# Gated linear attention on one core: the samples' tile first, their state updates spread over the prompt's tiles, and the conditioning matmuls in four column quadrants with half of them ahead

## The reference, cut to what matters

```
mod = jax.nn.silu(c) @ w_ada + b_ada            # [9, 1024] @ [1024, 6 * 1024]
sh1, sc1, ga1, sh2, sc2, ga2 = split(mod, 6)
h = rms_norm(x, g_mix) * (1.0 + sc1) + sh1      # sh1, sc1 are needed first
... q, k, v, r, a_low = split(h @ w_in) ...
# gated linear attention, 4 heads, keys of 64, values of 128, state S [64, 128] a head
S   = exp(sum log_a) * S + sum_t k_t v_t^T
o_t = q_t S_t ;  o = rms_norm(o) * silu(r)
x = x + ga1 * (concat(o_sb, o) @ w_out)         # ga1 and the rest are needed after it
```

## Time and profile before

| what | us |
|---|---|
| median of 3 runs (lowest, highest) | 2003.95 (2003.08, 2006.66) |
| the profiled execution, its own time | 2010.14 |
| its span in the profile | 2008.1 |
| PE busy in the span | 1770.6 (88%) |
| DVE busy, ACT busy, POOL busy | 706.4, 565.6, 405.2 |
| `stage_start`, up to the first matmul of the next stage | 0 to 80.3 |
| `stage_gla` | 844 to 1057.5 |

### The profile page before, as it was taken

The page is one execution under the profiler, slowest core; times in us unless marked ns, Lnnn a source line. Parts: engine busy times, 40 slices in busy tenths (PEclk is TensorE's granted clock), DMA queues, the critical chain, the costliest instruction groups (busy, mean ns, idle before and its releaser), DMA issues. The chain is left out here.

```text
span 2008.1 us, 26856 instructions
## 1 busy us (share of the span) xinstructions
PE 1770.6 (88%) x10388; PEld 1513.1 (75%) x10388; DVE 706.4 (35%) x1302; ACT 565.6 (28%) x1087; POOL 405.2 (20%) x293
## 2 busy tenths in 40 slices
PE   7799789999946888878867967999999999999996
PEld 1599778788834444423446967999999999999996
DVE  2300122322215777656550133323232323233334
ACT  3411021111115777633322133121213121212122
POOL 1011121122110000100001123232324242323230
PEclk9799989999977999979868988999999999999998
DMA  8121354554173000155405101111111111111102
GB/s 299 54 86 55 92 180 140 159 162 126 54 252 121 22 22 1 47 152 157 134 16 183 42 0 45 62 42 42 42 42 42 42 42 59 45 42 42 42 0 100
DMA packets 102739, 164.97 MB, mean 82 GB/s; under 512 B 7498, under 2 KB 55965, under 8 KB 102662
## 3 DMA queue, kind: packets, MB, share of 16 engines
q1 hardware_dynamic: 93952, 133.71, 20.6%
q0 software_dynamic: 5120, 16.78, 2.7%
q10 hardware_dynamic: 3590, 13.48, 1.7%
HBM read 138.18 MB, written 25.76 MB: 82 GB/s over the span
## 5 line engine op out<-in xcount | busy, mean ns | idle before, releaser
L376 PE MATMUL psum<-op_hi,out_hi 128*128 128x384 f32 (+1 forms) x960 | 319.8, 333 | 29.7 <-DVEq L2232 29.7
L378 PE MATMUL psum<-op_hi,out_lo 128*128 128x384 f32 (+1 forms) x960 | 314.8, 328 | 0.0
L377 PE MATMUL psum<-op_lo,out_hi 128*128 128x384 f32 (+1 forms) x960 | 314.8, 328 | 0.0
L378 PE MATMUL psum<-mlp_a_hi,out_lo 128*128 128x384 f32 (+1 forms) x768 | 250.9, 327 | 0.0
L377 PE MATMUL psum<-mlp_a_lo,out_hi 128*128 128x384 f32 (+1 forms) x768 | 250.6, 326 | 0.0
L376 PE MATMUL psum<-mlp_a_hi,out_hi 128*128 128x384 f32 (+1 forms) x768 | 250.4, 326 | 0.0
L376 PEld LDWEIGHTS psum<-op_hi,out_hi 128*128 128x128 f32 x960 | 181.8, 189 | 31.8 <-DVEq L2232 30.2
L2189 POOL TENSOR_TENSOR out_lo<-out_raw,out_hi 128x2048 fp32r<-128x2048 f32 x31 | 143.1, 4615 | 273.6 <-ACT out_hi L2209 273.6
L2238 DVE TENSOR_TENSOR mlp_sq<-mlp_relu 128x384 f32<-128x384 f32 (+1 forms) x96 | 88.3, 920 | 296.4 <-ACT mlp_relu L2222 296.4
L377 PEld LDWEIGHTS psum<-op_lo,out_hi 128*128 128x128 f32 x960 | 181.8, 189 | 1.6
L378 PEld LDWEIGHTS psum<-op_hi,out_lo 128*128 128x128 f32 x960 | 181.6, 189 | 0.0
(11 more groups left out here) (291 smaller groups left out, 2856.3 us busy)
## 6 DMA issues: line engine op xcount, KB each, us to landing
sa_k<-in_cache_k SPq DMA_DIRECT2D x64, 256.0 KB, 3.1
sa_v<-in_cache_v POOLq DMA_DIRECT2D x64, 256.0 KB, 3.8
ada_w<-in_w_ada SPq DMA_DIRECT2D x32, 512.0 KB
out_raw<-in_w_up SPq DMA_DIRECT2D x16, 1024.0 KB, 5.4
out_raw<-in_w_down SPq DMA_DIRECT2D x16, 1024.0 KB, 5.1
ada_w<-in_w_ada SPq DMA_DIRECT2D x4, 2048.0 KB, 12.4
projT<-in_stage ACTq DMA_DIRECT2D x12, 544.0 KB, 2.7
projT<-pg_stage ACTq DMA_DIRECT2D x12, 544.0 KB, 4.0
```

The lines of the kernel that those rows point to most:

```text
L376: pe.matmul(out, w_hi, x_hi, start=(k == 0), stop=False)
L377: pe.matmul(out, w_hi, x_lo, start=False, stop=False)
L378: return pe.matmul(out, w_lo, x_hi, start=False, stop=(k == nk - 1))
```

## The change

- `cT` is padded to 32 columns a slice (`QUAD` = 32). `condition` lets input slice k write to the PSUM partitions `32 * (k % 4)` onwards: four slices sum into four quadrants of one bank, two each. DVE or ACT then copies all 128 partitions, and `turn_rows` no longer transposes but multiplies the 128 rows with `gather` (128 x 9, four identities one below the other), which adds the four quadrants while it turns. POOL makes `gather` and zeroes `cT` at the start.
- In `stage_gla` a quarter is 512 rows x 256 columns (512 KB as before, in rows of 1 KB where they were 2 KB). The first `PRE` = 4 chunks, 16 quarters, are loaded and multiplied before the loop, through 6 buffers: the two own ones and four that alias tiles the loop uses later. A quarter is loaded once the last one in its buffer is used (`SLOT`). Chunks 4 to 7 are done in the loop, in the samples' tile and the first three of the prompt, through the two own buffers, and in two halves: quarters 0 and 1 before `turn_out`, quarters 2 and 3 after it. The copy of the rows moves from DVE to ACT, to the end of ACT's work for a tile.
- The samples' tile comes first: position n = 0 is tile 8, position n is tile n-1. `keys(n)` is that of prompt tile n and feeds `score(n+1)`; `outer` and `state` of a prompt tile move to `outer(n-1)`, `state(n-1)`. The samples' values and keys have buffers of their own (`vs`, `kns`). SP loads `S0` and the first `r` and `v` tiles behind the 16 quarters.
- The samples' states are updated in pairs at n = 5 to 8: `mask_keys(pair)` on DVE, `sample_outer(pair)` on PE (8 matmuls of 64 x 64 x 128, was 4 of 64 x 128 x 256, for two samples), `sample_states(pair)` on DVE one position later. Only the last pair's update lies behind the loop.
- Elsewhere buffers are only overlaid to make room.

```diff
-def condition(pe, g, bank, w, k0, n):
+def condition(pe, g, bank, w, k0, n, cols=slice(0, 512)):
 
     for k in range(k0, k0 + n):
-        last = pe.matmul(bank[0:NMOD, :], g.cT[:, k, :], w[:, k - k0, :], start=(k == 0), stop=(k == KD - 1))
+        q = k % 4 * QUAD
+        last = pe.matmul(bank[q:q + QUAD, cols], g.cT[:, k, :], w[:, k - k0, :], start=(k < 4), stop=(k >= 4),
+                         skip_group_check=True)
     return last
 
 
 def turn_rows(pe, g, bank, c0, rows):
 
     for m in range(4):
-        last = pe.transpose(bank[:, c0 + m * NMOD:c0 + (m + 1) * NMOD], rows[:, m * P:(m + 1) * P], g.ident[0:NMOD, 0:NMOD])
+        last = pe.matmul(bank[:, c0 + m * NMOD:c0 + (m + 1) * NMOD], rows[:, m * P:(m + 1) * P], g.gather[:],
+                         start=True, stop=True, skip_group_check=True)
...
+        own = [sb(f"ada2_w{i}", [P, 4, 256]) for i in range(2)]
+        wa = [t[:] for t in own] + [t[:].rearrange("p a h t -> p (a h t)").rearrange("p (k c) -> p k c", k=4) for t in (pt2, on2, fin2, sr2)]
+        arow = [sb(f"ada2_rows{i}", [P, 512]) for i in range(2)]
...
+        PRE = 4
+        PAIR_AT = {5: 0, 6: 1, 7: 2, 8: 3}
+        SLOT = [t % 6 if t < 4 * PRE else t % 2 for t in range(4 * NADA)]
...
+        ADA = [g.bank[b] for b in (7, 6, 5, 4, 7, 7, 7, 7)]
...
+                for i in range(4 * PRE):
                     weights(i)
+                sp.dma_start(vs[:], g.vgnat[tile(NT)]).then_inc(s_vs, 16)
                 sp.wait_ge(s_z, 4)
                 s0d = io["state_gla"][0].rearrange("s (m h) k v -> h m k s v", h=2)
                 for h in range(2):
                     for m in range(2):
                         sp.dma_start(s0[HALF[h], :, 2 * m + h, :], s0d[h, m]).then_inc(s_s0, 16)
+                load_r(0)
+                load_v(0)
+                load_r(1)
+                load_v(1)
+                load_r(2)
+                for n in range(2, N9):
+                    for i in range(4 * PRE + 4 * n - 8, min(4 * PRE + 4 * n - 4, 4 * NADA)):
+                        weights(i)
+                    if n > 2:
+                        load_r(n)
+                    if n < NT:
+                        load_v(n)
...
+                def ada_rows(i):
+                    act.wait_ge(s_am, 4 * i + 4)
+                    at_least(act, s_at, i - 1)
+                    act.copy(arow[i % 2][:], ADA[i]).then_inc(s_ar, 1)
...
+                ada_rows(3)
                 copy_kn(0)
+                for n in range(N9):
+                    if n < NT:
+                        key_exps(n)
+                    if n + 1 < N9:
+                        copy_kn(n + 1)
+                    gate_ln(n)
+                    norms(n)
+                    gate_exp(n)
+                    if n > 0:
+                        fin_hi(n - 1)
+                    if n + PRE < NADA:
+                        ada_rows(n + PRE)
...
+                dve.wait_ge(s_kn, 1)
+                for n in range(N9):
+                    if n < NT:
+                        keys(n)
+                    scores(n)
+                    gate_exponent(n)
+                    if n > 0:
+                        normed(n - 1)
+                    for i in {0: (2, 3), 1: (4,), 2: (5,), 3: (6,), 4: (7,)}.get(n, ()):
+                        ada_mod(i)
+                    if n == 4:
+                        scale_gain(dve, g, g.mul2, SC2, KD)
+                    if n > 0:
+                        if n > 1:
+                            dve.wait_ge(s_st, 4 * n - 4)
+                        state(n - 1)
+                    if n - 1 in PAIR_AT:
+                        sample_states(PAIR_AT[n - 1])
+                    if n in PAIR_AT:
+                        mask_keys(PAIR_AT[n])
+                    if n > 0:
+                        gated(n - 1)
+                sample_states(PAIR_AT[NT])
                 normed(NT)
                 gated(NT)
...
+                def sample_outer(pair):
+
+                    pe.wait_ge(s_km, 2 * pair + 2)
+                    pe.wait_ge(s_ae, NADA)
+                    pe.wait_ge(s_x, 1 + 8 * pair)
+                    for s in range(2):
+                        for m in range(2):
+                            for h in range(2):
+                                head, c0 = 2 * m + h, (2 * s + m) * GV
+                                last = pe.matmul(XP[HALF[h], c0:c0 + GV], kem[s][:, head * GK:(head + 1) * GK],
+                                                 vs[:, head * GV:(head + 1) * GV], start=True, stop=True, skip_group_check=True)
+                    last.then_inc(s_xp, 1)
 
                 ada(0)
+                for i in range(1, PRE):
+                    ada(i)
+                    turn_ada(i - 1)
                 pe.wait_ge(s_d, 13)
                 turn_keys(0)
                 score(0)
+                turn_ada(PRE - 1)
+
+                for n in range(N9):
+                    if n + 1 < N9:
+                        turn_keys(n + 1)
+                        score(n + 1)
+                    if 0 < n <= NADA - PRE:
+                        turn_ada(n + PRE - 1)
+                    output(n)
+                    if n > 0:
+                        outer(n - 1)
+                    if n + PRE < NADA:
+                        ada(n + PRE, (0, 1))
+                    if n > 0:
+                        turn_out(n - 1)
+                    if n + PRE < NADA:
+                        ada(n + PRE, (2, 3))
+                    if n in PAIR_AT:
+                        sample_outer(PAIR_AT[n])
                 turn_out(NT)
```

More of the change, by code:

```diff
@@ L181, in stage_start @@
         w = [sb(f"ada_w{i}", [P, KD, 512]) for i in range(2)]
-        rows = [sb(f"ada_rows{i}", [NMOD, 512]) for i in range(2)]
+        rows = [sb(f"ada_rows{i}", [P, 512]) for i in range(2)]
+        spare = sb("ada_silu_den", [P, KD, NMOD])
         vec = sb("ada_vec", [VEC_B + 6 * KD, P])
         x = [sb(f"n1_x{i}", [P, D]) for i in range(9)]
-        sq = sb("n1_sq", [P, D])
+        sq = hT_lo[:, 0, 0:D]
         ss = sb("n1_ss", [P, 9])
@@ L246, in _ @@
                 pool.tensor_copy(g.ident16[:], g.ident[:]).then_inc(s_const, 1)
+                pool.memset(g.gather[:], 0.0).then_inc(s_const, 1)
+                pool.memset(g.cT[:], 0.0).then_inc(s_const, 1)
+                for q in range(4):
+                    pool.wait_ge(s_const, 7 + q)
+                    pool.affine_select(out=g.gather[:], in_=g.gather[:], compare_op=ALU.not_equal, fill=1.0,
+                                       base=-q * QUAD, pattern=[[-1, NMOD]], channel_multiplier=1).then_inc(s_const, 1)
                 w_in.first_lo(pool)
@@ L704, in stage_project_gla_and_sample_attention @@
         w = [sb(f"sa_w{i}", [P, NPAGE, 4, QUAD]) for i in range(2)]
-        orow = [sb(f"sa_out_rows{i}", [P, P]) for i in range(2)]
         o = g.sample_o
@@ L1437, in weights @@
-                    sp.dma_start(wa[i % 2][:], part.rearrange("(k p) c -> p k c", p=P)).then_inc(s_wa[i % 2], 16)
-                for i in range(2):
-                    load_r(i)
-                for i in range(10):
+                    half, k = divmod(m, 2)
+                    c0 = 2 * D + chunk * 512 + half * 256
+                    part = io["w_ada"][0][k * 4 * P:(k + 1) * 4 * P, c0:c0 + 256]
+                    sp.dma_start(wa[SLOT[i]], part.rearrange("(k p) c -> p k c", p=P)).then_inc(s_wa[SLOT[i]], 16)
@@ new lines, in sample_states @@
+                def sample_states(pair):
+                    dve.wait_ge(s_xp, pair + 1)
+                    for s in (2 * pair, 2 * pair + 1):
+                        for h in range(GH):
+                            r = HALF[h % 2]
+                            c0 = (s % 2 * 2 + h // 2) * GV
+                            dve.scalar_tensor_tensor(out=s0[r, s, h, :], in0=s0[r, s, h, :], scalar=dec[r, h // 2, NT + s:NT + s + 1],
+                                                     in1=XP[r, c0:c0 + GV], op0=ALU.mult, op1=ALU.add).then_inc(s_x, 1)
```

304 lines of the change are left out of this document (124 added, 180 removed).

## The result

| | before | after |
|---|---|---|
| time, median of 5 runs | 2004.98 us (2003.08 to 2008.22) | 2016.16 us (2014.62 to 2019.09) |
| ratio, 95% interval | | 1.0055 [1.004, 1.007] |
| profiled execution, its span | 2010.14, 2008.1 us | 2014.62, 2013.0 us |
| first matmul of `project_in` | 80.30 us | 77.70 us |
| gated attention, DVE's first step to the next stage's first load | 845.50 to 1057.56, 212.1 us | 839.75 to 1062.99, 223.2 us |

The forecast was 2000.8 us, in a range of 1983 to 2010. The change takes 61 us from the conditioning's matmuls: they were 101.7 us and are now 41.0 us in 320 records. (The page's group of 240 records and 30.7 us leaves out the 80 whose quarters lie in the four aliased tiles.) The turns of the rows take 13.8 us more, 18.9 for 5.1. And the kernel is slower.

What follows compares the result with a forecast made beforehand. PE was taken to bound the kernel, busy 88% of the span, conditioning matmuls holding 101.7 us. Opening -7.8 and gated attention +4.6 sum to -3.2, from a median of 2003.95 to 2000.8 us; range 1983 to 2010.

Steps and rivals of the forecast that it cites:

- the quadrants' speed: Conditioning matmuls: quadrants overlap fully for f32, so a chunk takes 1.8 us at full clock, 3.5 at low.
- that rival: Conditioning: quadrants do not overlap at 256 or 512 columns, the opening gains nothing, 2027 us; chance 0.04.
- The opening, -7.8: Opening stage: ACT starts modulating x at 42.3 instead of 50.1, a gain of 7.8 us.
- bias and multiplier 0.9: Opening stage, DVE after chunk 3's turn: bias and multiplier together take 0.9 us.
- The prologue: Gated attention before position 1: about 10 us later than the old loop's start, sample tile included; output(0) ends at 899.6.
- Positions with conditioning, 20.0 us: Gated attention, samples' tile and n = 1 to 3: 20.0 us a position for 16.6, keys waiting on ACT.
- The wait does not form: Gated attention, n = 1 to 3: quarters 2 and 3 come early, positions take 17.3 us, 1992; chance 0.15.
- quarters late: Gated attention: quarters 2 and 3 arrive later than 3.85 us; at 5.9 us it is +8, 2009; chance 0.17.
- Positions without it: Gated attention's later positions: keys 7.8 us after outer, burst 9.0; a pair's updates, 3.0 us, lie on DVE's chain.
- Clock credit, 4 us: Gated attention: the clock returns before outer ends in some bursts, 0.5 us each, 4 us taken off in all.
- My slower rival: Gated attention: quarters 2 and 3 arrive later than 3.85 us, each microsecond costing four on ACT's chain; chance 0.17.
- Clock rivals: Gated attention: full clock holds in half the bursts, 1983 us, chance 0.15, or in all, 1970 us, chance 0.04.

Runs made afterwards that it cites:

- The opening alone: Changed opening stage with the gated attention of the kernel before: 2001.24 us, ratio to before 0.9967.
- POOL waiting: Kernel after, with POOL's subtraction of the first w_in panel waiting until DVE has done the multiplier: 2015.65 us, ratio to before 1.0045.
- the fillers: Kernel after with conditioning rows copied later on ACT, plus unread matmuls where PE waits in the gated attention: 1988.42 us, ratio to before 0.9905.
- The last order: Kernel after with rows' copy later, POOL's wait, next keys earlier, late quarters and samples' outer products behind the next score: 1971.69 us, ratio to before 0.9822.
- The gated attention alone: Changed gated attention with the opening's product and turn in whole rows as before: 2023.98 us, ratio to before 1.0078.
- the early keys: Kernel before, with the next tile's keys ahead of the state update on DVE and their exponentials ahead of ACT's norms: 2018.21 us, ratio 1.0046.

## Why the prediction was wrong, point by point

**What bounds the kernel, and the quadrants' speed: right.** A chunk of 8 matmuls takes 3.6 us at the low clock and 1.9 at the high (forecast 3.5 and 1.8), 3.7 times less than the 7.04 of whole rows at the high one. So the quadrants overlap nearly fully, and that rival is dead.

**The opening, -7.8: the mechanism right, the size 1.2 too large at best.** The opening alone measured -6.6 us. ACT's start was forecast for 42.3 and is 42.2 to 43.2 in four of six profiles: where PE waits for the chunk it lands at 37.8 to 38.7 instead of 36.4, and from the product's end to the bias it takes 1.9 us instead of 1.3, since two turns of 1.0 us stand there, one of them beside the copy. But the product ran at 2.4 GHz where I had taken 1.2, and the errors cancel: by luck. When the clock is as I took it, both errors stand (44.2, POOL waiting), and POOL adds 3.3 (47.5). The failed term is DVE's "bias and multiplier 0.9", taken from a timeline in which POOL was finished by then; pulled ahead by 6 to 8 us it met POOL's 4.5 us subtraction and was booked with 3.47 us for 0.23. The profile had that row, 5.76 us of POOL from 41.57; I read it as an idle engine's work. And of ACT's gain `project_in` keeps 5.8 to 6.7 of 6.9 to 7.9 us even at best, since `op_lo` meets POOL instead.

**The prologue: 3.3 us too short.** Score(2) was forecast 64.2 us from the stage's start (909.7 less 845.5) and came at 67.5. Most of it is there at the start of score(1), 42.1 for 39.0. The last quarter came at 34.4, forecast 32.0, and from it to the first keys 3.8 us passed where 3.1 were forecast: PE's product and a turn through `gather`, 1.88 us at the low clock, stand ahead of `turn_keys(0)`. The step that failed is that I took the quarters to be hidden and the copy of the samples' keys to come 1.1 us behind DVE's preparation; DVE waited 4.6 us for it. The run with the state held back puts 1.4 of the last quarter's 2.4 us down to the state's transfers, which I had put behind the quarters and which run beside them.

**Positions with conditioning, 20.0 us: right,** 20.1 to 20.4 between scores in this profile, 20.4 to 21.9 in three others of the same loop, and for the reason given: the wait of 2.9 us for quarter 2, the copy on ACT, the exponentials behind it. Moving the copy gives back 12.8 us over score(1) to score(6). "The wait does not form" and "quarters late" are out: quarter 2 is used 3.8 us after quarter 0 (920.84, quarter 0 done near 917.0), as in the earlier trace rows, not 5.9.

**Positions without it: right.** Between the ends of `outer` they take 16.4, 17.0 and 20.2 us for 16.8, 17.5 and 20.5. The state updates lie on DVE's chain nearly whole; moved behind the loop they cost only 5.7 us more.

**Clock credit, 4 us: wrong.** I took 0.5 us a burst, "some bursts will see the clock come back before `outer` ends". At n = 1 to 3 it does (the output's second product takes 1.5 to 1.8 us instead of 1.9, `outer` 1.03 instead of 1.9), but the turn through `gather`, 1.8 us in each of those bursts where I counted at most 0.5, takes that and more; from n = 5 on it came with the last instruction of a burst or behind it. Without the credit the forecast for the stage was 220.6 us. With the prologue's 3.3 it would have been 223.9, and 223.2 was measured in that profile (224.4 and 226.1 in two others with the same loop, where `outer` at n = 1 took 1.91 us and the clock came back later). These two terms, 7.3 us, are the error of the stage, +11.2 for +4.6; the others miss by 0.7 together.

**The sum.** -2.6 to -6.6 and +11.2 to +14 give 5 to 11 us, against -3.2. So the sign turned on the stage's two terms, 7.3 us, and the opening's 1 to 5. My slower rival had the right side and a wrong mechanism. A sum of -3.2 between terms of -7.8 and +8.6 (before the credit) bore no more than even chances of its sign. The stages say 5 to 11 us; the whole, 8 to 14 by its interval, lies at their upper end.

**Clock rivals.** Neither came by itself. What they would be worth is shown by the fillers, 18 us of the stage. The last order gets a part of the clock back by shortening PE's waits.

What stays open: why the profiled stages between differ by up to 9.5 us from run to run (762 to 772 us from `project_in` to the gated attention), and what sets the clock in the first bursts of the gated attention and in the opening. The gated attention alone, 15.7 us slower in time, fits its stage if that is held against the 210.7 us of the opening alone (+15.4), and less well against before's 212.1 (+14); its profiled execution was the slowest of its six, 9.7 us above their median.

## What to carry to other kernels

When a copy leaves a busy engine for one with room, ask what stands behind it in the new queue: here 0.6 us of copy on ACT, placed ahead of the next tile's exponentials, carried a DMA wait into the chain and cost 13 us, more than the whole loss. An engine made faster needs the waits in its order shortened too, or it idles and its clock goes down: the same quadrants lost 0.55% in the order as made and won 1.8% once keys, late quarters and masks stood where less waited behind them. The first step of that order, the early keys, lost 0.46% without the quadrants, as it was placed there; whether the full order needs them is not shown. And a step pulled ahead must be checked against what the other engines do at its new time, not at its old one.

## What the runs showed of the hardware

- A DVE instruction that meets a running POOL subtraction over 128 x 2048 is booked as one long instruction, 3.47 us for 0.23, 3.56 for 0.69, both with two inputs in SBUF. The timeline shows no wait there. A multiplier that started 0.3 us ahead of POOL, and had ended by then, took its 0.23.
- Matmuls whose result nobody reads, 2.7 us of them in a wait of 3, held the granted clock at 1.00 and made a burst from score to outer 5.4 us long instead of 9.2; behind an idle of 1.35 us it read 0.50 for nearly the whole next burst. Placed where PE waited 2.2 us or less, they cost 9 us.
- A turn of 128 rows through a 128 x 9 operand, eight records, takes 1.8 us at the low clock and 1.0 at the high. Its eight loads of 128 x 128 are booked with 1.83 us, where the four loads of 9 x 128 in the kernel before took 0.50. The loads fill the 1.82 us of the turn, so for so few columns the loading is the price.
- Two transfers of 512 KB issued ahead of 1 MB in four transfers on the same queue were used 6.3 and 8.6 us after their issue; with that 1 MB held back, 6.3 and 7.3. In the earlier trace rows a quarter took 3.85 us from the release of its buffer to its use; there two buffers were being filled, here six. That this is the cause is not shown.
